# The last MLP's down layers by seven products instead of eight, with token rows as output, and a last norm along those rows

## What is computed

```python
hm = rmsnorm(x, norm_mlp_g)                                   # x: 512 x 1024
x = x + jnp.square(jax.nn.relu(hm @ w_up)) @ w_down           # w_up 1024 x 4096, w_down 4096 x 1024
return rmsnorm(x, norm_final_g)                               # x * rsqrt(mean(x*x) + 1e-6) * g
```

## Time and profile before

| | us |
|---|---|
| time, median of 3 runs | 1600.73 (1599.74 to 1600.9) |
| profiled execution, first to last instruction | 1599.3 |
| of it PE busy | 1576.6 (99%) |
| DVE busy | 893.6 (56%) |
| ACT busy | 731.5 (46%) |
| POOL busy | 577.5 (36%) |
| MLP, first matmul of up0 to last of down3 | 249.1 |
| from there to the last instruction | 12.8 |

### The profile page before, as it was taken

One profiled execution on the slowest core, in us unless ns is written; L12 is line 12 of the kernel. 1 busy time (PEld: TensorE's weight loads), 2 busy tenths in 40 slices (PEclk: granted clock), 3 DMA queues, 4 the chain that ended last, 5 costly groups with the idle time before them and its releaser, 6 DMA issues.

```text
span 1599.3 us, 20589 instructions
## 1 busy us (share of the span) xinstructions
PE 1576.6 (99%) x7712; PEld 1286.2 (80%) x7712; DVE 893.6 (56%) x1164; ACT 731.5 (46%) x880; POOL 577.5 (36%) x237
## 2 busy tenths in 40 slices
PE   9999999999999999999999999999999999999997
PEld 7888888688888788888899778668868888888886
DVE  6366211782465799989876599654433642322314
ACT  5365222434345788887864432874243322222221
POOL 1422454134342233222224656343413434443441
PEclk9999999999999999999999999999999999999998
DMA  5421243222246899999964325102312223233221
GB/s 203 126 73 53 80 145 118 79 79 79 105 138 244 359 420 401 388 392 393 390 269 157 105 94 163 51 27 80 132 53 79 79 105 105 79 105 105 83 102 53
DMA packets 49762, 251.57 MB, mean 157 GB/s; under 512 B 9952, under 2 KB 12768, under 8 KB 23456
## 3 DMA queue, kind: packets, MB, share of 16 engines
q1 hardware_dynamic: 43344, 237.90, 40.6%
q0 software_dynamic: 5184, 8.40, 1.4%
q10 hardware_dynamic: 1168, 4.39, 0.7%
HBM read 235.05 MB, written 16.78 MB: 157 GB/s over the span
## 4 chain that ended last, share of the span: by engine, by line
PE 91%; DVE 3%; DMA 2%; ACT 2%; POOL 1%; issue 1%; SPq 0%; DVEq 0%; ACTq 0%
PE psum L233 26%; PE psum L235 26%; PE psum L234 26%; PE psum L2380 2%; PE psum L2415 1%; PE psum L1073 1%; PE psum L2403 1%; PE psum L1351 1%; POOL w_lo L149 1%; PE psum L2673 1%; DMA moe_w<-in_w_moe 1%; PE psum L723 1%; PE psum L2697 1%; PE psum L1052 1%; DMA k_mem_rows<-k_mem 1%
## 5 line engine op out<-in xcount | busy, mean ns | idle before, releaser
L149 POOL TENSOR_TENSOR w_lo<-raw,w_hi 128x2048 fp32r<-128x2048 f32 x90 | 414.7, 4607 | 647.3 <-ACT w_hi L143 612.4
L143 ACT ACTIVATE w_hi<-raw 128x2048 fp32r<-128x2048 f32 x95 | 181.5, 1911 | 318.5 <-PE psum L235 318.0
L233 PE MATMUL psum<-x_hi,w_hi 128*128 128x512 f32 (+1 forms) x816 | 316.3, 388 | 1.0 <-POOL w_lo L149 1.0
L234 PE MATMUL psum<-x_lo,w_hi 128*128 128x512 f32 (+1 forms) x816 | 314.1, 385 | 0.0
L235 PE MATMUL psum<-x_hi,w_lo 128*128 128x512 f32 (+1 forms) x816 | 314.1, 385 | 0.0
L1369 DVE TENSOR_TENSOR moe_lo<-moe_w,moe_hi 128x2048 fp32r<-128x2048 f32 x100 | 228.1, 2291 | 33.5 <-ACT moe_hi L1359 32.3
L1359 ACT ACTIVATE moe_hi<-moe_w 128x2048 fp32r<-128x2048 f32 x100 | 191.2, 1915 | 31.9 <-PE psum L235 18.3
L233 PEld LDWEIGHTS psum<-x_hi,w_hi 128*128 128x128 f32 x816 | 153.3, 188 | 33.4 <-issue 3.0
L234 PEld LDWEIGHTS psum<-x_lo,w_hi 128*128 128x128 f32 x816 | 153.3, 188 | 31.0 <-issue 0.7
L235 PEld LDWEIGHTS psum<-x_hi,w_lo 128*128 128x128 f32 x816 | 153.3, 188 | 30.7
L233 PE MATMUL psum<-y_hi,w_hi 128*128 128x512 f32 x352 | 137.9, 392 | 0.0
(11 more groups left out here) (401 smaller groups left out, 2842.1 us busy)
## 6 DMA issues: line engine op xcount, KB each, us to landing
raw<-in_w_dense SPq DMA_DIRECT2D x95, 1024.0 KB, 4.8
moe_w<-in_w_moe_ahead SPq DMA_DIRECT2D x54, 1024.0 KB, 13.9
moe_w<-in_w_moe SPq DMA_DIRECT2D x48, 1024.0 KB, 13.1
yrow<-expert_rows SPq DMA_DIRECT2D x8, 512.0 KB, 7.4
res<-in_x SPq DMA_DIRECT2D x4, 512.0 KB, 6.7
decay<-in_decay SPq DMA_DIRECT2D x8, 256.0 KB, 5.2
hn_rows<-hn_tok ACTq DMA_DIRECT2D x4, 512.0 KB, 5.7
out<-res SPq DMA_DIRECT2D x3, 512.0 KB, 2.6
```

The source lines that it names most:

```text
L143: act.activation(w_hi[c % RING][:, :], raw[c % RING][:, :], ACT.Copy).then_inc(hi_ready, 1)
L149: pool.tensor_tensor(w_lo[c % RING][:, :], raw[c % RING][:, :], w_hi[c % RING][:, :].bitcast(F32), ALU.subtract).then_inc(lo_ready, 1)
L233: pe.matmul(out, lh, rh, start=first, stop=False, **more)
L234: pe.matmul(out, lh, rl, start=False, stop=False, **more)
```

## The change

**Down layers.** The squared activations A (512 tokens x 1024 hidden) and the down weights B (1024 x 1024) of a group are cut into quarters, A into 256 x 512 parts and B into 512 x 512 parts. Seven products of quarters or of sums of quarters take the place of eight (Winograd's form of Strassen's method). A product is 2 row tiles x 4 x 3 = 24 matmuls of the same shape as before, so a down layer has 7 x 24 = 168. The activations are now the stationary operand and the weights the moving one, so the output has tokens on the partitions.
- Seven parts of A are wanted for each of four pieces of 128 hidden units `c`: four quarters less the one used only in sums, and S1 to S4. ACT squares into `f_parts`, DVE makes S1 to S4 (`sums`), ACT makes the high half of all seven in one copy of 128 x 1792 (`parts_high`), DVE the low half (`parts_low`).
- Four sums of weight quarters are made by DVE in place (`weights_1` to `weights_4`, 128 x 2048 each).
- A "unit" is a weight operand of 128 x 2048: seven a down layer, and the four chunks of an up layer. ACT makes the high half of each (`unit_high`), POOL the low half (`unit_lower`), but DVE makes those of units 2 and 3 of each group. There are three slots for the halves and four for raw weights.
- Products accumulate in PSUM where they share terms. DVE adds 14 row tiles a group to `res_t` (`add`).

**Order.** up0, down0, up1, down1, up2, down2, up3, down3: each down layer comes directly after the up layer that feeds it. `down` runs products 0 and 1 over the pieces 0 to 2 first and over piece 3 behind that.

**Residual stream.** `res` is turned into token rows by 32 transposes on PE inside up0 (`rows`), and eight copies by ACT out of PSUM.

**Last norm.** Rows have the features along the free dimension, so ACT squares and sums a row in one instruction; POOL multiplies by the gain, ACT and DVE by 1/rms. PE has no part in it. Four transfers of 512 KB store the result.

The diff, cut to its core (what it removes is printed above):

```diff
+    LOWERED_BY_VECTOR = (2, 3)
+    A11, A22, A12, S1, S2, S3, S4 = range(PRODUCTS)
+    BANKS_X, BANKS_Y, BANKS_Z = (1, 2), (4, 5), (3, 0)
+    UP_BANKS = (6, 7) + BANKS_Z
...
+    def wait_used(eng, U):
+        g, n = divmod(U, UNITS)
+        if n >= PRODUCTS:
+            eng.wait_ge(up_tile, KT * g + 2 * (n - PRODUCTS) + 2)
+        else:
+            eng.wait_ge(p_done, 2 * PRODUCTS * g + 2 * n + 2)
+    def unit_high(act, U):
+        if U >= 3:
+            wait_used(act, U - 3)
...
+        act.activation(unit_hi[(U + 2) % 3][:, :], unit_source(U)[:, :], ACT.Copy).then_inc(highs_done, 1)
+    def unit_lower(eng, U):
+        eng.wait_ge(highs_done, ONCE + U + 1)
+        eng.wait_ge(lows_done, ONCE + U)
+        eng.tensor_tensor(unit_lo[(U + 2) % 3][:, :], unit_source(U)[:, :], unit_hi[(U + 2) % 3][:, :].bitcast(F32),
+                          ALU.subtract).then_inc(lows_done, 1)
...
     def mlp_gpsimd(pool):
+        for U in range(1, UNITS * G - 4):
+            if U % UNITS not in LOWERED_BY_VECTOR:
+                unit_lower(pool, U)
+        done = 2 * PRODUCTS * (G - 1)
+        pool.wait_ge(gain_landed, ROWS_LANDED + 16)
+        for q in range(2):
+            pool.wait_ge(p_added, done + 9 + q)
+            pool.tensor_tensor(y_rows[q][:, S:D], res_t[q][:, S:D], gain_row[:, S:D], ALU.mult).then_inc(last_gained, 1)
+        for q in range(2, TB):
+            pool.wait_ge(p_added, done + 9 + q)
+            pool.tensor_tensor(y_rows[q][:, :], res_t[q][:, :], gain_row[:, :], ALU.mult).then_inc(last_gained, 1)
...
     def mlp_scalar(act):
+        for g in range(G):
+            U0 = UNITS * g
+            if g:
+                unit_high(act, U0 - 2)
+                squares(g, 0)
+                unit_high(act, U0 - 1)
+                parts_high(g, 0)
+                for c in range(1, 4):
+                    squares(g, c)
+                    unit_high(act, U0 + c - 1)
+                    parts_high(g, c)
+            for n in range(3, PRODUCTS + 2 * (g + 1 < G)):
+                unit_high(act, U0 + n)
...
     def mlp_vector(dve):
+        def sums(g, c):
...
+            dve.tensor_tensor(f_tmp[:, T_S3, :], f_tmp[:, T11, :], f_tmp[:, T21, :], ALU.subtract)
+            link(dve, dve.tensor_tensor(f_tmp[:, T_S1, :], f_tmp[:, T21, :], f_tmp[:, T22, :], ALU.add))
+            link(dve, dve.tensor_tensor(f_tmp[:, T_S2, :], f_tmp[:, T_S1, :], f_tmp[:, T11, :], ALU.subtract))
+            dve.tensor_tensor(f_tmp[:, T_S4, :], f_tmp[:, T12, :], f_tmp[:, T_S2, :], ALU.subtract).then_inc(f_summed, 1)
+        def parts_low(g, c):
+            dve.wait_ge(f_high, ONCE + 4 * g + c + 1)
+            dve.tensor_tensor(f_lo[c][:, :, :], f_tmp[:, 1:, :], f_hi[c][:, :, :].bitcast(F32), ALU.subtract)\
+               .then_inc(f_low, 1)
...
+        for g in range(G):
+            for c in range(4):
+                rectified(g, 2 * c)
+                if c == 2:
+                    weights_1(g)
+                if c == 3:
+                    weights_2(g)
+                rectified(g, 2 * c + 1)
+                sums(g, c)
+                parts_low(g, c)
+                if c == 2:
+                    weights_3(g)
+                if c == 3:
+                    unit_lower(dve, UNITS * g + 2)
...
+            add(g, 0, BANKS_X, 2, 0, -4)
+            add(g, 1, BANKS_Y, 0, 1, -3)
+            unit_lower(dve, UNITS * g + 3)
+            add(g, 2, BANKS_X, 2, 1, -2)
+            weights_4(g)
+            add(g, 3, BANKS_Z, 2, 0, 0)
+            add(g, 4, BANKS_X, 0, 1, 1)
...
     def mlp_tensor(pe):
+        def down(g):
+            product(g, 0, A11, BANKS_X, range(3), begins=True)
+            product(g, 1, S1, BANKS_Y, range(3), begins=True)
+            product(g, 0, A11, BANKS_X, (3,))
+            product(g, 1, S1, BANKS_Y, (3,))
+            product(g, 2, S2, BANKS_X, added=0)
+            product(g, 3, A12, BANKS_Z, begins=True)
+            product(g, 4, S3, BANKS_X, added=2)
+            product(g, 5, S4, BANKS_Y, added=1)
+            product(g, 6, A22, BANKS_X, added=4)
+        dense_pe(pe, "up0", x_hi, x_lo, norm=norm_mlp,
+                 hooks={0: lambda: norm_mlp.pe(pe), 1: first_rows, 2: lambda: rows(2)})
+        pe.wait_ge(rows_read, ONCE + 2 * TB)
+        for g in range(G):
+            if g:
+                up(g)
+            down(g)
```

More of the change, by code:

```diff
@@ L69 @@
           ("q_b", 2), ("k_b", 2), ("v_b", 2), ("out2", 4), ("q_cross", 4),
[L70 to L71 removed]
+          ("o_cross", 4), ("up0", 4)]
 TILES_OF = {"keys": 3, "sb_v": 8, "sb_out": 8, "ret_v": 16, "v_b": 8}
@@ L2715, in build @@
     G = 4
[L2716 to L2722, removed]
@@ L2773, in mlp_vector @@
[L2773 to L2778, removed]
-        norm_mlp.wait_inverted(dve)
[L2780 to L2816, removed]
@@ L2818, in mlp_tensor @@
-    def mlp_tensor(pe):
[L2819 to L2839, removed]
@@ new lines, in build @@
+    gain_row = at("last_gain_row", 48, [P, D])
+    y_rows = [at(f"y_rows{q}", 52 + 4 * q, [P, D]) for q in range(TB)]
+    sq_rows = [at(f"sq_rows{b}", 68 + 4 * b, [P, D]) for b in range(2)]
+    right_sum, right_mean, row_sum, row_rms, row_rstd = (
+        at(f"last_{n}", 204 + i / 32, [P, TB]) for i, n in enumerate(("right_sum", "right_mean", "sum", "rms", "rstd")))
+    up_tile, up_relu, p_done, p_added = (sem("mlp_" + n) for n in ("tile", "relu", "product", "added"))
+    f_squared, f_summed, f_high, f_low, highs_done, lows_done, t_added, rows_turned, rows_read, last_right = (
+        gdif_done, gexp_done, edif_done, eexp_done, both_done, rank_done, hot_done, lists_done, lgt_read, lgt_done)
@@ new lines, in build @@
+    last_squared, last_mean, last_rooted, last_inverted, last_gained, last_left = u_high, u_low, s_high, s_low, tr_done, tr_read
+    m_landed, X_LANDED = x_landed, 16
+    gain_landed, stored, ROWS_LANDED = yrows_landed[0], yrows_landed[1], 32
+    ONCE = 1
+    slots = [[2, 3, 0, 1]]
+    for _ in range(G - 1):
+        a0, a1, a2, a3 = slots[-1]
+        slots.append([a3, a1, a2, a0])
+    nth_load, _loads = {}, [0] * 4
+    for g in range(G):
+        for what in ("up", "down"):
+            for k in range(4):
+                if (g, what) != (0, "up"):
+                    _loads[slots[g][k]] += 1
+                    nth_load[what, g, k] = _loads[slots[g][k]]
@@ L2967, in _layout, with quarters @@
     }
-    for g in range(4):
-        parts[f"up{g}"] = wu[:, g * D:(g + 1) * D]
-        parts[f"down{g}"] = wd[g * D:(g + 1) * D, :]
+    parts["up0"] = wu[:, :D]
+    def quarters(w):
+        q = w.reshape(4, 2, P, 2, S).transpose(1, 3, 2, 0, 4).reshape(2, 2, P, CHUNK_COLS)
+        return np.stack([q[0, 0], q[0, 1], q[1, 1], q[1, 0]])
+    w_mlp = [quarters(wd[:D])]
+    for g in range(1, 4):
+        w_mlp += [_chunks(wu[:, g * D:(g + 1) * D]), quarters(wd[g * D:(g + 1) * D])]
     w_dense = np.concatenate([_by_rows(parts[n]) if n in ("sb_v", "v_b") else _chunks(parts[n], 4 if n == "sb_out" else KT)
@@ L3046 @@
         d[name] = nc.dram_tensor(f"in_{name}", a.shape, mybir.dt.from_np(a.dtype), kind="ExternalInput").ap()
-    d["out"] = nc.dram_tensor("out", [P, KT, S], F32, kind="ExternalOutput").ap()
+    d["out"] = nc.dram_tensor("out", [S, D], F32, kind="ExternalOutput").ap()
     build(nc, d)
```

289 lines of the change are left out of this document (242 added, 47 removed).

## The result

| | before | after |
|---|---|---|
| median of 5 runs each, on one chip, us | 1600.32 (1599.42 to 1600.90) | 1606.54 (1604.88 to 1607.22) |
| ratio | | 1.0034, 95% interval 1.0022 to 1.0046 |
| span of the profiled execution | 1599.3 | 1603.7 |

The account below looks back on a forecast made before the run. PE's number of dense matmuls was taken as the bound. 1599.3 - 21.8 (matmuls) + 3.5 (transposes) + 18.8 (stalls) - 3.5 (tail) = 1596.3 us of span, plus 1.4 for the median: 1597.7, range 1584 to 1606.

Parts of the forecast that it names:

- Matmuls removed: Down layers: each goes from 192 to 168 matmuls at 0.2267 us, 21.8 us less over four layers.
- Transposes: up0: 32 transposes added on PE cost 3.5 us.
- Durations of what is new: New DVE and ACT instructions: `parts_low` 2.02 us, `parts_high` 1.70, DVE's 128 x 256 0.42, four of `sums` 1.6.
- POOL holds DVE, and the chain to the last piece: Down layers: POOL holds `parts_low`, so PE stalls 4.35 us in groups 1 to 3, 5.7 in group 0; 18.8 in all.
- second date: Rival: behind the stall PE also waits, above all for product 2's first `add`; some 2.3 us twice a group, 1607; chance 0.05.
- The first two rivals: Down layers: holds miss the chain, no stall, 1577.5 (chance 0.08); or part of the stall, 2 us a group, 1588 (0.17).
- Whether DVE holds POOL too: POOL behind `weights_4`: full hold taken, delaying POOL 2.0 us off PE's path; without it 1.8 us less, tail only.
- The tail: From the last dense matmul's slot to the end: 9.3 us instead of 12.8, 3.5 less.
- The sum without the clock: Whole kernel, stalls at their length and clock kept: 1596.3 us of span; chance 0.45 for 1594.5 to 1600.
- The clock: Rival, down layers: stalls drop PE's clock, 1.6 us lost in each of four groups, 1604.1; at double that 1610.5; chance 0.25.
- Clock falls in some or all stalls: Down layers: the forecast's case of PE's clock dropping in the stalls, 1599 to 1610 us, chance 0.25.
- Runs above the span: Whole kernel: the runs' median lies 1.4 us above the span, giving 1597.7 from 1596.3.

Follow-up runs that it names:

- the kernel with 14 idle matmuls: Changed kernel plus 14 matmuls with unused results on PE before piece 3 in each down layer, filling part of the pause; 1598.03 us, 0.9981 of the kernel before.
- the kernels whose pause is filled: Changed kernel plus 14 or 19 matmuls with unused results on PE before piece 3 in each down layer; 1598.03 and 1598.15 us, spans 1596.4 and 1596.5.

## Why the prediction was wrong, point by point

- *Matmuls removed.* Right: 38.21 us for 168 where nothing disturbs them, up layers unchanged at 43.52.
- *Transposes.* Right: up0 47.99 us, forecast 47.9; each group of 16 took 1.7 us, 3.3 for both against 3.5.
- *Durations of what is new.* Right: `parts_low` 2.03 (2.02), `parts_high` 1.70 (1.70), a part of `sums` 0.42 to 0.43 (0.42).
- *POOL holds DVE, and the chain to the last piece.* Right in place and size: 4.37 us in groups 1 to 3 (forecast 4.35), 0.7 and 4.93 in group 0 (0.85 and 4.9). The queues of up1 and down1 went as followed: `parts_low` of pieces 1, 2 and 3 ended at T + 31.7, 44.15 and 55.9 (31.7, 44.2 and 55.8), and PE started 0.14 later. Agreement to 0.02 us is partly luck all the same, as the terms printed for piece 3 add up to T + 56.0, a stall of 4.6. Cutting short the two POOL instructions removed the pause, and moving them to DVE left 0.5 us. No second date was missed: PE had no other new wait. The first two rivals are out. (Two sums beside the forecast are off: DVE's share per group is 28.2 us by its terms, not 28.5, and the rival of a second date, two waits of 2.3 us a group, would come to 1616 and not 1607.)
- *Whether DVE holds POOL too.* Fully, as taken. In the timeline of down2, POOL's two halves and `weights_4`:

```profile
1482.94 11.27 POOL L2797 TENSOR_TENSOR unit_lo<-mlp_raw,unit_hi 128x2048 fp32r<-128x2048 f32 x2 [22.33 <-DVE unit_lo L2797]
...
1485.99 3.71 DVE L2979 TENSOR_TENSOR mlp_raw<-mlp_raw,mlp_raw 128x2048 f32<-128x2048 f32 x1
```

  Two POOL halves of 4.61 take 11.27 us together, 2.05 more: `weights_4` got in between them. By the Trainium skill, SBUF — State Buffer, "Who interferes with whom", whoever issues first has the pair of ports for the whole instruction. The traces agree in both directions, to 0.1 us.
- *The tail.* 9.3 forecast, 8.76 in the kernel with 14 idle matmuls, 8.05 in the changed one. The term was 0.5 too large; the other 0.7 is no merit, as POOL was that much further ahead of a slowed PE: its last gain product ended 0.85 us before the matmuls' end, against 0.08 with 14 idle matmuls, and its three low halves before them took 16.02 us in both.
- *The sum without the clock.* 1596.3 us of span forecast, 1596.4 and 1596.5 in the kernels whose pause is filled. Small errors cancel (the passages behind the pauses 1.0 more, the tail 0.5 less, an up0 that began 0.3 earlier), but the queues and holds were read rightly.
- *The clock.* Here the prediction failed, in two steps. The forecast's sum has the four stalls at their length alone, with the clock kept. It gave "Clock falls in some or all stalls" 0.25, with the argument that "the fall needn't hit each stall, and the level may come back sooner". It hit all four, and in the other kernels all nine pauses of 4.8 us or more too. And the rival sized the loss as half of 3.2 us, 1.6 a group: the lower level lasted 4.7 to 5.6 us into the work, and the loss was 2.0 to 2.5 us a group, 9.3 in all against 6.4. The forecast should have stood where this rival did, with the measured size at 1596.3 + 9.3 = 1605.6 of span. What remains to the 1603.7 measured is the tail (1.2 less), an MLP that began 1.6 us earlier in that execution, and the passages (1.0 more).
- The evidence was at hand: the clock had fallen 3.2 us after the last dense matmul, and the forecast pauses were longer. There was no row of a dense stage with a pause over 1.6 us in which the clock had held. The argument against had no row. The Trainium skill, TensorE: Matmul & The Clock Gate, "Why this matters for your kernels", would have had all four stalls hit, and the trace agrees; but its bound of about 3 us is not safe here, where 2.2 to 2.7 us cost clock three times out of four.
- *Runs above the span.* I took 1.4 us. The profiled execution took 1605.47, 1.8 above its span, and the median another 1.1 above that.

Open: why one of three equal pauses of 2.2 us cost nothing, and why equal pauses of 7.04 us lost from 1.4 to 2.8 us. Between 1.6 and 2.2 us nothing was tried.

## What to carry to other kernels

A pause that a change opens in a dense row of matmuls can cost more than its length: here 4.4 us of waiting took 2.3 to 2.5 us more in clock, so that waiting that looked as if it would just be paid for by fewer matmuls (21.8 us saved) turned into a loss. If the wait can't be removed, matmuls that do nothing can keep the clock (here 8.4 us back, and no date missed); better is to find whose instruction holds the producer. When DVE does arithmetic on two SBUF operands beside POOL, count POOL's whole instruction as DVE's time unless DVE comes first, look where the hold lands in DVE's queue before reordering, and weigh moving the work to DVE, where it takes half as long (2.29 against 4.61 us) and here left PE pauses of 0.5 us. It isn't free of holds: DVE holds POOL too.
